# One fused block of two transformer layers plus a recurrent layer: start-up loads, first attention and the compression matmuls in another order

## The chip, the cores and the metric

The kernel runs on one core of a Trainium2 chip. The metric is the device time of one execution in microseconds (us), the median of several runs. TensorE (PE) does the matmuls and the transposes, VectorE (DVE) and ScalarE (ACT) the elementwise work, GpSimd (POOL) some of it, and the queues of SyncE (SP) and of ACT issue the transfers between HBM and the on-chip memory. All engines run their own instruction lists and meet at semaphores.

## The reference, cut to what matters

The input is 256 tokens of 1024 features, float32. The part that the change touches is the first mixer, `even_mixer`:

```
parts = split(hn @ w_in)           # q, kc, vc, ks, vs, kw, vw, g, dq, dk, dv
kc = compress_kv(kc, pos_k, w1_k, w2_k)    # 15 compressed keys and values per head group:
vc = compress_kv(vc, pos_v, w1_v, w2_v)    # gelu(window of 32 tokens @ w1) @ w2
gates = sigmoid(g)
o_a = nsa_attention(q, kc, vc, ks, vs, kw, vw, gates, bias)   # 8 heads, sum of three branches
o_b = diff_attention(dq, dk, dv, lam, subln_g, bias)          # 4 heads, rms_norm of the result
return concatenate([o_a, o_b]) @ w_out
```

Then come a squared-relu MLP, a second mixer (block attention, 16 heads), a second MLP, and a second block with a recurrence, another attention and a gated feed-forward. None of these is touched.

## The kernel before, in words

Every dense matmul is done in split precision. A weight slab of 1024 x 256 is loaded by SP into one of five places of `raw` (`RING = 5`); ACT copies it to `w_hi` in a rounded format (`split_hi`, L683), DVE subtracts to get `w_lo` (`split_lo`, L1023), and PE's `gemm` (L1561) does three products for each of 8 chunks and each of two halves: 48 matmuls for a slab, 6 for a chunk. ACT splits a slab three slabs ahead of its use (`AHEAD`), DVE two. The results lie in two PSUM buffers that alternate by group number. ACT or DVE must empty one before the second next group is written.

The first stage projects the normalised x by twelve slabs, in this order: KV_CMP, Q0, SKW, GATE, SV, DQ0, DK0, DQ1, DK1, DV0, DV1, Q1. GATE has 24 columns only. KV_CMP is the input of the compression, a chain of small float32 matmuls: two sets (k and v) of 16 with 45 columns each, then ACT's gelu, then three matmuls of `compress()`, then DVE's copies into `kc` and `vc`. Before, PE does the 16 of k behind the chunks of SV (two behind each), the 16 of v behind those of DQ0, and `compress()` after DK0.

The start: SP loads x, then the slabs up to SV, then the compression weights `cw1`, small things, and the slabs from DQ0 on. ACT's queue first issues the loads of `norm_mix`, of the bias table, and 18 small loads of parameters (`par_rows`, L765 and L767). Then it writes 16 copies of a row of bias values to HBM (L772), and when they have landed (`brow_out`) it loads from them the 2 MB tile `nb`, the bias of every head by query and key (L778): eight loads, each for the 16 partitions a, a+8, a+16, ... Behind those in ACT's order stands `root(0)` (L699), the square root for the first norm, on which DVE's `inv_rms` (L1035) and all evictions wait.

`attention(0)` is a loop over steps i with a software pipeline. In step i, PE does the transposes of pair i-2 (L1640), the values of pair i-3 (L1655), the scores of pair i (L1628), and then what the table `FILL` gives for the step: whole slabs or halves of slabs of the projections ("in"), or chunks of the output projection that are ready ("out"). DVE does `logits(i)` (L1063), then `normalise(i-1)` (L1092), and ACT the exponentials (L740) and the copies of the transposes (L723). There are 16 pairs in the first attention: for each of four head pairs two full ones (branches over all keys and over the window) and one compressed ("cmp", 15 keys), and four of the differential attention. Its rms_norm is done in steps 10 to 14 ("dn"): sums of squares on PE (L1674) and a square root on ACT in step 10, a reciprocal on DVE in step 11, 8 broadcasts on PE (L1685) in step 12, the product on DVE (L1105) and the split into high and low in steps 13 and 14.

Of the kernel before, what the change touches and what calls it, by code (L numbers as in the profile page):

```python
# [12 lines left out]
P = 128  # L13
# [35 lines left out]
    {0: [("in", DQ0, 0, 8)], 1: [("in", DK0, 0, 8)], 2: [("in", DQ1, 0, 8)], 3: [("in", DK1, 0, 8)], 4: [("in", DV0, 0, 4)],  # L49
     5: [("in", DV0, 4, 8)], 6: [("in", DV1, 0, 4)], 7: [("in", DV1, 4, 8)], 8: [("in", Q1, 0, 4)], 9: [("in", Q1, 4, 8)],  # L50
     14: [("out", 0, (0,)), ("out", 1, (0,))], 15: [("out", 0, (1, 4)), ("out", 1, (1, 4))],
     16: [("out", 0, (5, 6)), ("out", 1, (5, 6))], 17: [("out", 0, (7, 2)), ("out", 1, (7, 2))]},
# [12 lines left out]
IN_BEFORE = (5, 2, 6)  # L65
# [75 lines left out]
def build(nc, ctx, t, out):  # L141
# [210 lines left out]
    def att_pairs(p):  # L352
# [10 lines left out]
        if p == 0:  # L363
# [3 lines left out]
            def nsa(hp):  # L367
                heads, g = (2 * hp, 2 * hp + 1), hp // 2
                end, vg = CMP_BLOCK - 1, vc[:, g * HD:(g + 1) * HD]
                for b in range(2):  # L370
                    v = [sv[:, tb, b * P + g * HD:b * P + (g + 1) * HD] for tb in range(TB)]
                    pairs.append(dict(
                        kind="full", gate=8 * (b + 1) + 2 * hp, out=hp, start=(b == 0), stop=False, last=False,
                        units=[unit(aq[r, hp, :], skw[r, b, g, :], [nb[:, h, P:T], nb[:, h, :]])
                               for h, r in zip(heads, halves)],
                        pv=[full_pv(v)] * 2, qk_groups=(grp[Q0 if hp < 2 else Q1], grp[SKW]), v_groups=(grp[SV],)))
                pairs.append(dict(
                    kind="cmp", gate=2 * hp, out=hp, start=False, stop=True, last=True,
# [5 lines left out]
                    qk_groups=(g0 + CMP2_GROUP,), v_groups=()))  # L384
# [78 lines left out]
    def _(sp):  # L463
# [27 lines left out]
        for j in range(DQ0):  # L491
            a_slab(j)
        for i, name in enumerate(("k", "v")):
            sp.dma_start(cw1[:, i, :, :], t[f"ev_cmp_w1_{name}"][0].rearrange("(m p) j -> p m j", p=P)).then_inc(ld["cw"], 16)
        sp.wait_ge(xt, 4)
# [180 lines left out]
    def _(act):  # L676
# [31 lines left out]
        def attention(p, in_slab):  # L708
            a, pairs, probs_t = att[p], PAIRS[p], prob_ts[p // 2]
            n = len(pairs)  # L710
            for i in range(n + 3):
# [39 lines left out]
                if p == 0 and i == DN_STEP + 3:  # L751
# [8 lines left out]
        for name, (tile, row, n) in PARAMS.items():  # L760
            if name != "norm_mix":
                src, letters = t[name], " ".join("abcd"[:len(t[name].shape)])
                if len(src.shape) > 1:
                    src = src.rearrange(f"{letters} -> ({letters})")
                act.dma_start(prow[row:row + n, tile, :], src[0:n * P].rearrange("(r c) -> r c", c=P)).then_inc(ld["par"], 16)  # L765
        tail = t["conv_f_w_2"].rearrange("a b c -> (a b c)")[P * P:144 * P].rearrange("(r c) -> r c", c=P)
        act.dma_start(prow[CONV_F_TAIL[1]:CONV_F_TAIL[1] + 16, CONV_F_TAIL[0], :], tail).then_inc(ld["par"], 16)  # L767
# [14 lines left out]
        def a_slab(j, opens=True, closes=True):  # L782
# [11 lines left out]
            if j == DQ0:  # L794
                compress()
# [13 lines left out]
        for j in range(DQ0):  # L809
            a_slab(j)  # L810
        act.wait_ge(lam_ok, 1)
# [196 lines left out]
    def _(dve):  # L1008
# [42 lines left out]
        def attention(p, in_slab):  # L1051
# [889 lines left out]
```

## Time and profile before

| | |
|---|---|
| median of 3 runs | 1222.54 us (1221.37 to 1222.99) |
| the profiled execution | 1222.54 us, its span 1220.7 us, 1.8 us around it |
| busy: PE, DVE, ACT, POOL | 1155.7, 794.5, 587.8, 147.3 us |
| mean granted clock of TensorE | 0.969 |
| on the chain that ended last | PE 79%, DVE 10%, DMA 3%, ACT 3%, POOL 2% |

Times in the rows are microseconds from the start of the span. In a timeline or chain, a row is start, duration, engine, line, operation; "ACTq" and "SPq" are the queues that issue transfers, and a bracket at a row's end is the idle time ahead of it with what ended it. In a table of stretches the columns are busy time (and instructions) of PE, PE's weight loads, DVE, ACT and POOL, then the granted clock of TensorE as a share of 2.4 GHz, the share of the DMA engines, and GB/s. The span's first 180 us hold the part that the change touches.

### The profile page before, as it was taken

Reading aid. Unit: us, or ns where it says so; the run is one execution under the profiler, and the core shown is the slowest. Engines: PE = TensorE matmul, PEld = TensorE weight load, DVE = VectorE, ACT = ScalarE, POOL = GpSimd, SP = SyncE. Lnnn points to the kernel's source line nnn. Section 1 sums busy time; section 2 is a strip of 40 time slices with the busy share of each in tenths; the row PEclk is TensorE's granted clock in tenths of the full one; section 3 lists DMA queues with packets and bytes.
Section 4 is the critical chain, followed back from the end, with each engine's and each line's share of the span. In section 5 each row is a group of like instructions: output and inputs, shape, how many; then the busy total and the mean of one; then the engine's idle time right before and its main releaser. Section 6 shows DMA issues by size and latency. Waiting matters only on the chain.

```text
span 1220.7 us, 21634 instructions
## 1 busy us (share of the span) xinstructions
PE 1155.7 (95%) x9407; PEld 1111.2 (91%) x9407; DVE 794.5 (65%) x1131; ACT 587.8 (48%) x824; POOL 147.3 (12%) x83
## 2 busy tenths in 40 slices
PE   6899899999999999999999999999977979999997
PEld 5898679999998999999999989999975879999997
DVE  5647548775546565877543978875554678888842
ACT  4257645444334555444334465663354446665531
POOL 3000012000220003000022201400050030111000
PEclk9699799999999999999999999999988999999999
DMA  9733125655654544565565362555941444566550
GB/s 279 202 114 124 40 66 177 186 194 177 200 177 141 168 141 139 173 190 190 179 200 175 97 210 70 173 161 182 314 137 35 138 139 139 176 198 197 193 187 35
DMA packets 198770, 195.71 MB, mean 160 GB/s; under 512 B 9691, under 2 KB 196756, under 8 KB 198676
## 3 DMA queue, kind: packets, MB, share of 16 engines
q1 hardware_dynamic: 191360, 188.43, 48.6%
q10 hardware_dynamic: 7316, 5.91, 1.9%
q8 instruction: 74, 1.21, 0.4%
q14 instruction: 20, 0.16, 0.0%
HBM read 192.86 MB, written 1.46 MB: 159 GB/s over the span
## 4 chain that ended last, share of the span: by engine, by line
PE 79%; DVE 10%; DMA 3%; ACT 3%; POOL 2%; issue 2%; ACTq 1%; DVEq 0%; POOLq 0%
PE ps_gemm L1561 70%; PE ps_score L1628 2%; PE ps_out L1655 2%; DVE w_lo L1023 2%; PE ps_trans L1640 2%; DMA f_bias<-cum_scr 2%; PE ps_score L1850 2%; DVE prob L1063 1%; POOL f_bias L642 1%; DVE xc L1334 1%; DVE prob L1092 1%; ACTq L778 1%; PE ps_gemm L1726 1%; DVE rs L1035 1%; ACTq L765 1%
## 5 line engine op out<-in xcount | busy, mean ns | idle before, releaser
L1561 PE MATMUL ps_gemm<-act_hi,w_hi 128*128 128x256 f32 x1640 | 463.3, 284 | 19.1 <-ACT act_hi L957 6.7
L1561 PE MATMUL ps_gemm<-act_hi,w_lo 128*128 128x256 f32 x1640 | 458.3, 281 | 0.0
L1561 PE MATMUL ps_gemm<-act_lo,w_hi 128*128 128x256 f32 x1640 | 446.3, 281 | 0.0
L1023 DVE TENSOR_TENSOR w_lo<-raw,w_hi 128x2048 fp32r<-128x2048 f32 (+2 forms) x179 | 408.4, 2290 | 51.4 <-ACT w_hi L683 51.1
L683 ACT ACTIVATE w_hi<-raw 128x2048 fp32r<-128x2048 f32 (+2 forms) x179 | 332.6, 1862 | 187.6 <-DMA raw<-in_mlp_w 97.1
L1561 PEld LDWEIGHTS ps_gemm<-act_hi,w_hi 128*128 128x128 f32 x1640 | 311.2, 190 | 27.6 <-issue 17.5
L1561 PEld LDWEIGHTS ps_gemm<-act_hi,w_lo 128*128 128x128 f32 x1640 | 310.8, 190 | 0.2
L1561 PEld LDWEIGHTS ps_gemm<-act_lo,w_hi 128*128 128x128 f32 x1640 | 302.6, 188 | 1.5
L1561 PE MATMUL ps_gemm<-hid_lo,w_hi 128*128 128x256 f32 x512 | 143.1, 280 | 0.0
L1561 PE MATMUL ps_gemm<-hid_hi,w_lo 128*128 128x256 f32 x512 | 143.1, 280 | 0.0
L1561 PE MATMUL ps_gemm<-hid_hi,w_hi 128*128 128x256 f32 x512 | 142.8, 279 | 0.0
L1561 PEld LDWEIGHTS ps_gemm<-hid_lo,w_hi 128*128 128x128 f32 x512 | 96.2, 188 | 0.0
L1561 PEld LDWEIGHTS ps_gemm<-hid_hi,w_hi 128*128 128x128 f32 x512 | 96.0, 188 | 0.0
L1561 PEld LDWEIGHTS ps_gemm<-hid_hi,w_lo 128*128 128x128 f32 x512 | 95.9, 187 | 0.0
L740 ACT ACTIVATE prob<-prob,nmin 128x128 f32<-128x128 f32 (+3 forms) x128 | 54.3, 425 | 34.8 <-DVE nmin L1063 34.6
L608 POOL TENSOR_TENSOR sq_sum<-x 128x512 f32<-128x512 f32 x5 | 12.8, 2570 | 466.8 <-DVE x L1228 236.0
L828 ACT ACTIVATE hid_hi<-up_r 128x512 fp32r<-128x512 f32 x32 | 20.3, 634 | 93.3 <-DVE up_r L1246 93.3
L1561 PE MATMUL ps_gemm<-w_hi,act_hi 128*128 128x256 f32 (+1 forms) x192 | 57.4, 299 | 0.0
L1561 PE MATMUL ps_gemm<-w_lo,act_hi 128*128 128x256 f32 (+1 forms) x192 | 55.6, 290 | 0.0
L1561 PE MATMUL ps_gemm<-w_hi,act_lo 128*128 128x256 f32 (+1 forms) x192 | 55.6, 289 | 0.0
L1063 DVE CUSTOM_DVE_ANT_0 prob<-ps_score,bias 128x128 f32<-128x128 f32 (+1 forms) x96 | 25.6, 323 | 45.0 <-PE ps_score L1628 44.8
L1561 PE MATMUL ps_gemm<-w_hi,h_hi 128*128 128x256 f32 x192 | 53.1, 277 | 0.0
(282 smaller groups left out, 1733.4 us busy)
## 6 DMA issues: line engine op xcount, KB each, us to landing
raw<-in_mlp_w SPq DMA_DIRECT2D x64, 1024.0 KB, 5.3
raw<-in_w_in SPq DMA_DIRECT2D x30, 1024.0 KB, 5.5
raw<-in_w_up SPq DMA_DIRECT2D x24, 1024.0 KB, 5.3
raw<-in_od_w_in SPq DMA_DIRECT2D x12, 1024.0 KB, 5.1
raw<-in_w_down SPq DMA_DIRECT2D x12, 1024.0 KB, 5.3
raw<-in_ev_w_in SPq DMA_DIRECT2D x9, 1024.0 KB, 6.2
raw<-in_w_proj_a SPq DMA_DIRECT2D x8, 640.0 KB, 4.3
raw<-in_ev_w_out SPq DMA_DIRECT2D x4, 1024.0 KB, 5.5
```

Source lines behind the costliest of these rows:

```text
L608: ins = pool.tensor_tensor(dst, v, v, ALU.mult)
L642: link(pool.tensor_tensor(nb2[:, :, c0:c0 + n], nb2[:, :, c0:c0 + n], fcq[:, b, :].unsqueeze(2).to_broadcast([P, 16, n]), ALU.subtract))
L683: act.activation(w_hi[:, slot, 0:k, 0:n], raw[:, slot, 0:k, 0:n], ACT.Copy).then_inc(hi_done, 1)
L740: ins = act.activation(v, v, ACT.Exp, scale=-1.0, bias=nmin[:, k, b:b + 1], accum_out=psum_[:, k, b:b + 1])
L828: act.activation(hid_hi[:, 2 * j:2 * j + 2, :], up_r[:, j % 2, :, :], ACT.Square).then_inc(hid_h, 1)
L1023: dve.tensor_tensor(w_lo[:, slot, 0:k, 0:n], raw[:, slot, 0:k, 0:n], w_hi[:, slot, 0:k, 0:n].bitcast(F32), ALU.subtract).then_inc(w_ready, 1)
L1063: ins = dve.tensor_tensor_reduce(out=prob[:, k % PB, c0:c0 + w], in0=ps_s[:, m, c0:c0 + w], in1=u["bias"][b], scale=1.0, scalar=u["init"], ...
L1561: ins = pe.matmul(dst, lhs, rhs, start=(first and opens and i == 0), stop=(last and closes and i + 1 == len(order)), skip_group_check=True)
L1628: ins = pe.matmul(ps_s[:, m, c0:c0 + w], u["q"][:, b * P:(b + 1) * P], u["k"][b], start=True, stop=True)
L1640: ins = pe.transpose(ps_t[0:w, 0 if pr["kind"] == "diff" else m, q * P:(q + 1) * P], prob[:, k, c0:c0 + w], ident[:, :])
L1655: ins = pe.matmul(ps_o[r, pr["seq"] % 2, o0:o1], v, probs_t[0:k, m, c0:c1], start=(pr["start"] and q == 0), stop=(pr["stop"] and q == 1), ...
L1850: ins = pe.matmul(ps_s[:, j % 2, i * T:(i + 1) * T], gw[:, i, c, j - c + 1, :], xc[:, c, :], start=(q == 0), stop=(q == len(srcs) - 1))
```

## The change

It has five parts.

1. The 18 small loads of parameters go from ACT's queue to SP's, behind the slabs KV_CMP, Q0 and SKW; the two loads of `cw1` (1 MB each) now come ahead of the slabs GATE and SV.
2. The eight loads of `nb` are each for 16 neighbouring partitions.
3. All 32 small matmuls of the compression run behind the chunks of SV, four behind each. DQ0 is projected ahead of the attention, and `compress()` comes right after it (`IN_BEFORE` 5 to 6).
4. In the first attention the compressed pair of a head pair comes first of its three, not last. `FILL` is shifted: inputs in steps 0 to 8, outputs in steps 13 to 17.
5. The differential norm's reciprocal stands ahead of the logits of step 11 and its broadcasts are in step 11; what follows moves up a step.

```diff
@@ FILL, first attention
-    {0: [("in", DQ0, 0, 8)], 1: [("in", DK0, 0, 8)], 2: [("in", DQ1, 0, 8)], 3: [("in", DK1, 0, 8)], 4: [("in", DV0, 0, 4)],
+    {0: [("in", DK0, 0, 8)], 1: [("in", DQ1, 0, 8)], 2: [("in", DK1, 0, 4)], 3: [("in", DK1, 4, 8), ("in", DV0, 0, 4)],
...
-     14: [("out", 0, (0,)), ("out", 1, (0,))], 15: [("out", 0, (1, 4)), ("out", 1, (1, 4))],
-     16: [("out", 0, (5, 6)), ("out", 1, (5, 6))], 17: [("out", 0, (7, 2)), ("out", 1, (7, 2))]},
+     13: [("out", 0, (0, 1)), ("out", 1, (0, 1))], 14: [("out", 0, (4, 5)), ("out", 1, (4,))],
+     15: [("out", 1, (5, 6))], 16: [("out", 0, (6, 7)), ("out", 1, (7,))], 17: [("out", 0, (2,)), ("out", 1, (2,))]},
@@ sync
-        for j in range(DQ0):
+        for j in range(3):
             a_slab(j)
+        for name, (tile, row, n) in PARAMS.items():
...
+                sp.dma_start(prow[row:row + n, tile, :], src[0:n * P].rearrange("(r c) -> r c", c=P)).then_inc(ld["par"], 16)
...
         for i, name in enumerate(("k", "v")):
             sp.dma_start(cw1[:, i, :, :], ...).then_inc(ld["cw"], 16)
+        a_slab(GATE)
+        a_slab(SV)
@@ scalar
-        for a in (0, 4, 1, 5, 2, 6, 3, 7):
-            src = bass.AP(tensor=scr_w.tensor, offset=P - 1 - a, ap=[[16 * REL - 8, 16], [REL, 16], [1, T]])
-            act.dma_start(nb[a:P:8, :, :], src).then_inc(nb_in, 16)
+        for a in range(P // 16):
+            src = bass.AP(tensor=scr_w.tensor, offset=P - 1 - 16 * a, ap=[[16 * REL - 1, 16], [REL, 16], [1, T]])
+            act.dma_start(nb[16 * a:16 * a + 16, :, :], src).then_inc(nb_in, 16)
@@ vector, step i of the first attention, ahead of logits(i)
+                if p == 0 and i == DN_STEP + 1:
+                    g = st["a_in"].g0 + DN_GROUP
+                    dve.wait_ge(emptied[g % 2], out_count(g))
+                    dve.reciprocal(dn_rs[:, :], dn_sd[:, :]).then_inc(dn["r"], 1)
@@ tensor
-                if p == 0 and i == DN_STEP + 2:
+                if p == 0 and i == DN_STEP + 1:
                     pe.wait_ge(dn["r"], 1)
...
+        def compress_chunk(k):
...
+            for m in range(4 * (k % 4), 4 * (k % 4) + 4):
+                i = k // 4
                 ins = pe.matmul(ps_g[:, b, i * T:i * T + 3 * NC].rearrange("p (g c) -> p g c", g=3), cw1[:, i, m, :],
...
-        a_slab(SV)
+        a_slab(SV, between=compress_chunk)
+        a_slab(DQ0)
+        compress()
         pe.wait_ge(rst_ok, 1)
```

What stands in a row on PE around the first two chunks of SV, before (a chunk's last matmuls, the small ones of the compression, the next chunk):

```order
L1561 MATMUL ps_gemm<-w_lo,act_hi 128x256
L1726 MATMUL ps_gemm<-cmp_in,cmp_w_86 128x45 x2
L1561 MATMUL ps_gemm<-w_hi,act_hi 128x256
L1561 MATMUL ps_gemm<-w_hi,act_lo 128x256
L1561 MATMUL ps_gemm<-w_lo,act_hi 128x256
```

and after:

```order
L1564 MATMUL ps_gemm<-w_lo,act_hi 128x256
L1735 MATMUL ps_gemm<-cmp_in,cmp_w_86 128x45 x4
L1564 MATMUL ps_gemm<-w_hi,act_hi 128x256
L1564 MATMUL ps_gemm<-w_hi,act_lo 128x256
L1564 MATMUL ps_gemm<-w_lo,act_hi 128x256
```

The small matmuls of both sets are now inside SV; the slab DQ0 has none.

PE after the last chunk of the slab ahead of the attention's first step, before (the first scores are those of a full pair, and DQ0 is the fill):

```order
L1726 MATMUL ps_gemm<-cmp_in,cmp_w_86 128x45 x2
L1628 MATMUL ps_score<-a_skw,a_q 128x128 [waits emptied0,emptied1,rst_ok]
L1628 MATMUL ps_score<-a_skw,a_q 128x128
L1628 MATMUL ps_score<-a_skw,a_q 128x256 x2
L1561 MATMUL ps_gemm<-act_hi,w_hi 128x256 [waits emptied0,w_ready]
```

and after (end of DQ0, then `compress()`, whose result `kc` the first scores read):

```order
L1564 MATMUL ps_gemm<-act_hi,w_lo 128x256
L1747 MATMUL ps_gemm<-cmp_hid,cmp_w_94 128x30 [waits emptied1]
L1749 MATMUL ps_gemm<-cmp_w_94,cmp_hid 15x64 x2
L1631 MATMUL ps_score<-kc,a_q 128x7 [waits emptied1,rst_ok]
L1631 MATMUL ps_score<-kc,a_q 128x7
L1631 MATMUL ps_score<-kc,a_q 128x15 x2
L1564 MATMUL ps_gemm<-act_hi,w_hi 128x256 [waits emptied0,w_ready]
```

The first scores moved behind DQ0 and behind DVE's copies of the compressed keys.

## Rows read from the trace of the kernel before

**Rows 1.** The page, granted clock of TensorE in 40 slices, tenths.

```profile
PEclk9699799999999999999999999999988999999999
```

**Rows 2.** The chain that ended last, first 40 us: start, us, what.

```profile
2.13 0.62 ACTq L765
...
9.40 0.44 ACTq L767
...
12.37 5.76 DMA bias_wide_scr<-bias_row
18.15 0.63 ACTq L778
...
23.52 2.75 ACTq L778
...
28.10 1.76 DVE rs L1035
...
36.03 14.83 PE ps_gemm L1561 x96
```

**Rows 3.** Timeline of ACT, splits of slabs 0, 5, 6 and the gates.

```profile
11.17 1.91 ACT L683 ACTIVATE w_hi<-raw 128x2048 fp32r<-128x2048 f32 x1
...
43.87 1.91 ACT L683 ACTIVATE w_hi<-raw 128x2048 fp32r<-128x2048 f32 x1 [11.95 <-DMA raw<-in_ev_w_in]
46.78 1.91 ACT L683 ACTIVATE w_hi<-raw 128x2048 fp32r<-128x2048 f32 x1 [1.00 <-DMA raw<-in_ev_w_in]
50.92 1.28 ACT L705 ACT_TABLE_LOAD   x1 [2.23 <-PE ps_gemm L1561]
```

**Rows 4.** Timeline of SP's queue: the issue of slab GATE.

```profile
9.52 3.15 SPq L472 DMA_DIRECT2D raw<-in_ev_w_in  x1
```

**Rows 5.** Timeline of POOL: the mask on the bias tile.

```profile
41.20 2.09 POOL L620 TENSOR_SCALAR_AFFINE_SELECT bias<-bias 128x2048 f32<-128x2048 f32 x1 [22.06 <-DMA bias<-bias_wide_scr]
```

**Rows 6.** Busy time and granted clock by stretch, 31 to 60 us.

```profile
31.00:36.00 5.00, 0.15 (x1) 0.03 (x2) 4.88 (x10) 0.92 (x1) 0.00 (x0) 0.63 1.13 249
36.00:40.00 4.00, 3.97 (x22) 4.00 (x23) 3.81 (x16) 0.00 (x0) 0.00 (x0) 0.61 1.15 259
...
48.00:52.00 4.00, 4.00 (x20) 4.00 (x19) 3.77 (x7) 1.77 (x2) 0.00 (x0) 0.50 0.05 12
...
56.00:60.00 4.00, 4.00 (x22) 4.00 (x22) 0.00 (x0) 0.00 (x0) 0.00 (x0) 0.55 0.00 0
```

**Rows 7.** The chain through SV and DQ0, 52 to 75 us.

```profile
52.73 1.09 PE ps_gemm L1726 x4
53.81 1.42 PE ps_gemm L1561 x6
55.23 0.71 PE ps_gemm L1726 x4
...
59.98 0.75 PE ps_gemm L1561 x6
60.73 0.39 PE ps_gemm L1726 x4
...
64.58 0.86 PE ps_score L1628 x8
...
74.81 0.86 PE ps_score L1628 x8
```

**Rows 8.** The chain through the later steps of the first attention.

```profile
128.74 0.66 PE ps_trans L1640 x6
...
142.23 3.71 PE ps_gemm L1685 x16
...
173.36 0.61 PE ps_out L1655 x8
```

**Rows 9.** The page, DVE's splits and logits: busy, mean ns of one, idle before.

```profile
L1023 DVE TENSOR_TENSOR w_lo<-raw,w_hi 128x2048 fp32r<-128x2048 f32 (+2 forms) x179 | 408.4, 2290 | 51.4 <-ACT w_hi L683 51.1
...
L1063 DVE CUSTOM_DVE_ANT_0 prob<-ps_score,bias 128x128 f32<-128x128 f32 (+1 forms) x96 | 25.6, 323 | 45.0 <-PE ps_score L1628 44.8
```

More of the change, by code:

```diff
@@ L369, in nsa @@
                 end, vg = CMP_BLOCK - 1, vc[:, g * HD:(g + 1) * HD]
[L370 to L376, printed above, removed]
                 pairs.append(dict(
-                    kind="cmp", gate=2 * hp, out=hp, start=False, stop=True, last=True,
+                    kind="cmp", gate=2 * hp, out=hp, start=True, stop=False, last=False,
                     units=[dict(q=aq[r, hp, :], k=[kc[r, g, 0:NC0], kc[r, g, :]], blocks=[(0, NC0), (P, NC)],
@@ L383, in nsa @@
                     pv=[[(vg[0:NC0, :], NC0, (0, P), (0, P)), (vg[0:NC, :], NC, (P, T), (P, T))]] * 2,
-                    qk_groups=(g0 + CMP2_GROUP,), v_groups=()))
+                    qk_groups=(grp[Q0 if hp < 2 else Q1], g0 + CMP2_GROUP), v_groups=()))
+                for b in range(2):
+                    v = [sv[:, tb, b * P + g * HD:b * P + (g + 1) * HD] for tb in range(TB)]
+                    pairs.append(dict(
+                        kind="full", gate=8 * (b + 1) + 2 * hp, out=hp, start=False, stop=(b == 1), last=(b == 1),
+                        units=[unit(aq[r, hp, :], skw[r, b, g, :], [nb[:, h, P:T], nb[:, h, :]])
+                               for h, r in zip(heads, halves)],
+                        pv=[full_pv(v)] * 2, qk_groups=(grp[SKW],), v_groups=(grp[SV],)))
             def diff(h):
@@ L750, in attention @@
                         .then_inc(emptied[g % 2], 1)
-                if p == 0 and i == DN_STEP + 3:
+                if p == 0 and i == DN_STEP + 2:
                     for g in (st["a_in"].g0 + DN_GROUP + 1, st["a_in"].g0 + DN_GROUP + 2):
@@ L759, in _ @@
         act.dma_start(btab[:, :], t["bias_table"]).then_inc(ld["bias"], 16)
[L760 to L767, printed above, removed]
         split_hi(0)
@@ L793, in a_slab @@
                     if j == GATE else NS)
-            if j == DQ0:
-                compress()
         def compress():
@@ L1108, in attention @@
                     normalise(i - 1)
-                if p == 0 and i == DN_STEP + 1:
-                    g = st["a_in"].g0 + DN_GROUP
-                    dve.wait_ge(emptied[g % 2], out_count(g))
-                    dve.reciprocal(dn_rs[:, :], dn_sd[:, :]).then_inc(dn["r"], 1)
                 for part in FILL[p].get(i, ()):
@@ L1121, in attention @@
                         .then_inc(a["ol"], 1)
-                if p == 0 and i == DN_STEP + 4:
+                if p == 0 and i == DN_STEP + 3:
                     dve.wait_ge(dn["hi"], 1)
@@ L1178, in a_slab @@
             ins.then_inc(emptied[g % 2], 1)
-            if j == DK0:
-                compress()
         def compress():
@@ L1219, in _ @@
         ins.then_inc(lam_ok, 1)
+        a_slab(DQ0)
+        compress()
         dve.wait_ge(lam_e, 1)
@@ L1713, in _, with a_slab @@
         g0 = st["a_in"].g0
-        def a_slab(j, k0=0, k1=KS):
+        def a_slab(j, k0=0, k1=KS, between=None):
             s, g = st["a_in"].s0 + j, g0 + A_GROUPS[j]
-            gemm(s, g, act_hi, act_lo, before_chunk=x_in(0) if j == 0 else None, low_last=j == 0,
-                 between={SV: compress_k, DQ0: compress_v}.get(j), tok_major=j in (DV0, DV1, SV, GATE),
-                 n=GATES if j == GATE else NS, ks=range(k0, k1), opens=k0 == 0, closes=k1 == KS)
-            if j == DK0:
-                compress()
-        def compress_part(i, k):
-            b = (g0 + CMP1_GROUP) % 2
-            for m in (2 * k, 2 * k + 1):
+            gemm(s, g, act_hi, act_lo, before_chunk=x_in(0) if j == 0 else None, low_last=j == 0, between=between,
+                 tok_major=j in (DV0, DV1, SV, GATE), n=GATES if j == GATE else NS, ks=range(k0, k1), opens=k0 == 0,
+                 closes=k1 == KS)
+        def compress_chunk(k):
+            g = g0 + CMP1_GROUP
+            b = g % 2
+            if k == 0:
+                pe.wait_ge(emptied[b], gwait(g))
+                pe.wait_ge(ld["cw"], 16 * 6)
+                gi = g0 + A_GROUPS[KV_CMP]
+                pe.wait_ge(emptied[gi % 2], out_count(gi))
+            for m in range(4 * (k % 4), 4 * (k % 4) + 4):
+                i = k // 4
                 ins = pe.matmul(ps_g[:, b, i * T:i * T + 3 * NC].rearrange("p (g c) -> p g c", g=3), cw1[:, i, m, :],
@@ L1768, in _ @@
         a_slab(GATE)
-        a_slab(SV)
+        a_slab(SV, between=compress_chunk)
+        a_slab(DQ0)
+        compress()
         pe.wait_ge(rst_ok, 1)
```

24 lines of the change are left out of this document (10 added, 14 removed).

## The prediction, made before the changed kernel ran

> **What bounds the kernel now.** I read the page first: PE is the chain for four fifths of the span, and its granted clock is at full level nearly everywhere except in the second and the fifth slice (0.6 and 0.7), and twice late in the program [rows 1]. A slice is 30.5 us, so the two are 31 to 61 and 122 to 153 us, and that is where the change works. Behind the first attention, from some 178 us on, nothing differs, so the sum is made up to there.
>
> Next the chain of waits for the first 40 us [rows 2]. ACT's queue issues 18 parameter loads (2.13 to 9.84, first and last of 18 rows), the bias row goes to HBM and is back at 18.1, eight loads of the bias tile are issued until 26.3, and only then come ACT's table load and square root (1.8 us). DVE's reciprocal starts at 28.1, and PE starts slab SKW at 36.03, 7.9 us behind the root. PE had next to nothing to do from 31 to 36 [rows 6].
>
> Then the timeline of ACT from 40 us on [rows 3]. The splits of slabs 5 (DQ0) and 6 (DK0) start when their transfers land, at 43.87 and 46.78: up to there the DMA engines are the limit (their share is 1.1 in [rows 6]). The gates are evicted at 50.92, behind PE's slab GATE. They stand in ACT's order behind the split of DK0.
>
> Last the clock with the chain [rows 6, 7]. From 48 to 60 us PE is busy all the time, and still at 1.2 GHz or little over it. The slab before was GATE, whose products have 24 columns. In SV, 6 products of a chunk take 1.42 us and the 2 small matmuls behind them 0.71 us (4 records); at 59.98 the same are 0.75 and 0.39 us. So the clock came back about 7 us into SV, where dense work is two thirds of the time at the low clock.
>
> **Part 1, the start.** ACT is rid of 18 issues, 7.7 us, but could not have used much of it: the split of slab 0 begins at 11.17 [rows 2, 3], the bias row is written by DVE at 12.3 behind PE, and the write to HBM issues at 12.37 all the same. What can change is its landing (5.76 us, beside SP's slabs) and the issue of the eight loads: six take 0.63 each, the last 2.75 as its queue is full [rows 2]. Eight times 0.64 would be 5.1 us instead of 8.1. So the root comes between 0 and 4 us earlier (1 for the landing, 3 for the issue), I take 2: SKW starts at about 34.
>
> This does not reach the gates. The issue of parameters on SP, 18 times 0.43 or 7.7 us, now stands between SKW and `cw1`. SP's queue is blocked by its backlog at 9.5 [rows 4], so that the DMA engines have work for some 6 to 7 us more; then they run short for about 1.3 us. All bytes up to DK0 are the same, thus DK0 lands at 46.78 + 1.3 = 48.1. Its split 1.9, table load 1.28, gates 0.45: 51.8. The first small matmul of the compression needs the buffer of GATE; it ran at 52.73 [rows 7]. Gain 0.9 us. The bounds: 3.9 if the DMA engines never run short and the new shape of the bias loads lets the slabs land 1.7 earlier, minus 3 if that shape hinders them.
>
> The mask on the bias ended at 43.3 [rows 5]; the first logits move to about 82 us, so the bias tile itself has 35 us of cover.
>
> **Part 2, the compression inside SV.** At the low clock a chunk of SV becomes 1.42 + 2 x 0.71 = 2.84 us: half of the time is dense, where it was two thirds. Before, the clock stayed down for 7 us of the denser mix. I take it that it stays down for all of SV: from the first small matmul on, 8 x 1.42 (small) + 7 x 1.42 = 21.3 us, against 64.58 - 52.73 = 11.85. That is +9.45. DQ0 is then without small matmuls: 8 x 0.75 = 6.0 at the full clock, 11.4 at the low. It begins low and recovers inside; I take 7.3 (a recovery after some 3 us of dense work, as behind 36 us, where the stretch 36 to 40 has a mean of 0.61 [rows 6]). Before it took 74.81 - 64.58 - 0.86 = 9.37. That is -2.07.
>
> Two waits are new. DQ0 writes the buffer that SV leaves, which ACT empties in 0.84 us; before, the scores of 0.86 us lay there: +1.0. The first scores read `kc`, which DVE copies behind the eviction of DQ0: +0.6. `compress()` itself is in both.
>
> The Trainium skill, page "TensorE: Matmul & The Clock Gate", section "What's actually happening", says that activity releases the throttle and that a sustained busy stretch brings the full clock. Taken by PE's busy time alone, SV (no gaps) would be at 2.4 GHz early; the row for 48 to 60 us shows PE busy without a gap at 0.50 to 0.55, so here the rule holds only if dense work counts. That is the second rival.
>
> **Part 3, the attention.** In steps 0 to 8 PE does the same less DQ0, with one short step: step 2 has half a slab (4 chunks of 0.75 and some 1.3 us of the pairs' own matmuls) against DVE's logits (four of 0.32), about as much for the normalisation, and a split of 2.29 [rows 9], 5.0 us: +0.7. Unfilled steps are four in both (10 to 13 before, 9 to 12 after), and both have the same products. The reciprocal ahead of the logits of step 11 is no stall: the square root is ready about when PE's scores of that step are. The 8 broadcasts (3.71 us at the low clock [rows 8]) now lie beside the logits of a full pair, where they cost less. But step 15 has 12 matmuls (1.5 us) against 2.8 of DVE (logits and normalisation): +1.3, and the clock falls a step sooner, in step 10. Before, steps 10 to 18 took 128.74 to 173.97 [rows 8]. I take +2.0 for all of this, with -2 and +4 as ends.
>
> **Sum.** -0.9 + 9.45 - 2.07 + 1.0 + 0.6 + 2.0 = +10.1 us. The profiled execution took 1222.54 us, which is the median too: 1232.6 us.
>
> **The rivals.**
> *The clock comes back in SV* as it did before, 7 us in. Then SV is 6.8 us at the low clock, a third of its 21.3, and two thirds of 11.6 us (15 groups at 0.75 to 0.78) at the full one: 14.6, +2.75 for +9.45. DQ0 is 6.0, -3.4. The sum is -0.9 + 2.75 - 3.4 + 1.6 + 2.0 = +2.0: 1224.6 us. For it: the mix of SV and DQ0 kept its short times from 59.98 on, up to the end of DQ0 [rows 7]. Against it: that was a clock already up, and a denser mix.
>
> *Faster.* The same, and the start is passed on: DK0 lands early, gates are ready with PE, 3.5 us for 0.9, and the attention's last steps gain 1.5 rather than lose 2, since the clock falls less there than in the fifth slice before. 1222.5 + 2.0 - 2.6 - 3.5 = 1218.4 us. For it: PE had 5 idle us at 31 to 36. Against: the landings.
>
> *The new shape of the bias loads hinders the slabs.* The eight loads took from 18.15 to 41.2 for 2.1 MB, 91 GB/s, beside the slabs [rows 2, 5]. If each now holds up the other queue, DK0 lands 4 us later, on top of the forecast: 1236.6 us. It decides from 1.8 us on, as the gates have little less in hand than this. The Trainium skill, "SBUF — State Buffer", section "Door 1: The DMA port swizzle", says that 16 neighbouring partitions reach four ports (104 GB/s at 1 MiB), where strided ones reach more. By that rule alone the eight need 20 us, not more than they took; only the crowding would cost.
>
> **How the numbers follow.** Forecast 0.54, clock back in SV 0.20, faster 0.16, hindered 0.10. A difference of 0.2% (2.4 us) is what can be told from none. The forecast and the last are slower; the second is around the edge, most of it within; so faster 0.18, same 0.18, slower 0.64. The range holds the second case and most of the faster: 1217 to 1238 us. The forecast's own is 1228 to 1236.
>
> **What would show it.** In the table of stretches, PE's granted clock through SV (about 52 to 73 us) at 0.50 with PE busy; the first small matmul at 51 to 53 us; SKW started at 33 to 35; the first scores near 83 us, where before those of step 1 were at 74.81 [rows 7]; a DMA share under 1 for a moment near 17 us. Wrong would be a clock of 1.00 before 62 us, a first small matmul outside 49 to 55, or a length of the attention off by more than 4 us from the sum of part 3.

## The result: 1241.55 us, 1.6 to 1.8% slower

The changed kernel took 1241.55 us (median of 4 runs, 1241.38 to 1241.62), against 1222.0 us before (median of 4): 1.6% more. The ratio on record, 1.0178 (interval 1.0165 to 1.0193), takes in all 29 executions of the changed kernel: 24 further ones took 1241.8 to 1246.7 us, and the median of all is 1244.1. The forecast was 1232.6 us and its range ended at 1238. The direction was right and the size was outside the range. In the profiled executions (1222.54 and 1240.8 us) the span grew from 1220.7 to 1239.0 us. Both kernels have 9407 matmuls, so the 18.3 us are waits and a lower clock. Read first the granted clock of the page, beside that of before [rows 1]:

```profile
PEclk9659989999999999999999999999988998999999
```

The second slice stayed at 0.6, the third (62 to 93 us) fell to 0.5, where it had been 0.9. The fifth rose. So the loss is in the first 95 us, and a little comes back later.

Why is the clock low for so long? First, all of it begins late. ACT's timeline gives the splits of slabs DQ0 and DK0 and the table load of the gates, as in [rows 3]:

```profile
56.93 1.91 ACT L694 ACTIVATE w_hi<-raw 128x2048 fp32r<-128x2048 f32 x1 [6.32 <-DMA raw<-in_ev_w_in]
59.94 1.91 ACT L694 ACTIVATE w_hi<-raw 128x2048 fp32r<-128x2048 f32 x1 [1.10 <-DMA raw<-in_ev_w_in]
61.87 1.28 ACT L716 ACT_TABLE_LOAD   x1
```

Both slabs land 13.1 us later than before (43.87 and 46.78). The table load stands behind DK0's split in ACT's order; before, it came 2.2 us behind that split, released by PE, and now it follows at once. So the landing of DK0 sets the eviction of the gates, and this frees the buffer that the first small matmul of the compression writes. SP's queue shows what it did meanwhile (start, us, then the load that it issued):

```profile
9.05 2.79 SPq L499 DMA_DIRECT2D par_rows<-in_norm_mlp  x1
...
20.97 0.52 SPq L501 DMA_DIRECT2D par_rows<-in_conv_f_w  x1
...
23.01 9.67 SPq L503 DMA_DIRECT2D cmp_w<-in_ev_cmp_w_v  x1
32.73 8.07 SPq L473 DMA_DIRECT2D raw<-in_ev_w_in  x1
40.85 3.51 SPq L486 DMA_DIRECT2D raw<-in_ev_w_in  x2
44.40 1.19 SPq L509 DMA_DIRECT2D cmp_w<-in_ev_cmp_w_k  x2
...
48.48 0.43 SPq L512 DMA_DIRECT2D small<-in_b_forget  x1
48.95 8.66 SPq L473 DMA_DIRECT2D raw<-in_ev_w_in  x4
```

The parameter loads occupy SP for 12.4 us (9.05 to 21.49). GATE, which was issued at 9.52 before [rows 4], is issued at 32.73; DQ0 at 48.95. The table of stretches (busy time of PE, PEld, DVE, ACT, POOL, then granted clock, DMA share and GB/s) shows what the DMA engines did with it:

```profile
16.00:20.00 4.00, 4.00 (x33) 4.00 (x33) 4.00 (x7) 0.00 (x0) 2.46 (x2) 0.92 0.62 97
20.00:30.00 10.00, 8.33 (x64) 7.62 (x63) 9.80 (x13) 3.56 (x3) 0.00 (x0) 1.00 1.16 122
...
48.00:52.00 4.00, 4.00 (x21) 4.00 (x20) 2.20 (x9) 1.91 (x1) 0.00 (x0) 0.50 0.24 50
...
72.00:76.00 4.00, 4.00 (x21) 4.00 (x21) 0.00 (x0) 0.00 (x0) 0.00 (x0) 0.50 0.00 0
...
92.00:96.00 4.00, 3.31 (x34) 3.12 (x32) 1.19 (x5) 0.00 (x0) 0.00 (x0) 1.00 0.09 11
```

There are two different losses here. At 16 to 20 and 48 to 52 us the engines had little to do (share 0.62 and 0.24). From 20 to 30 us they were fully busy (1.16) and moved 122 GB/s, while before moved, in the same stretch and also fully busy:

```profile
20.00:30.00 10.00, 9.65 (x77) 8.99 (x75) 5.48 (x7) 3.69 (x4) 0.00 (x0) 1.00 1.11 272
```

The chain from the first small matmul to the first scores (start, us, what), beside [rows 7]:

```profile
63.67 1.94 PE ps_gemm L1735 x8
65.61 1.42 PE ps_gemm L1564 x6
67.03 1.57 PE ps_gemm L1735 x8
...
84.94 1.57 PE ps_gemm L1735 x8
86.51 8.12 PE ps_gemm L1564 x48
...
95.78 0.62 PE ps_score L1631 x8
```

Eight chunks, each of six wide matmuls at 1.42 us and eight small ones at 1.57 us, none at the short times that [rows 7] has from 59.98 on: 22.84 us at a clock of 0.50, with PE busy without a gap (72 to 76 us above).

**The ledger**, by the prediction's own terms. The attention ends where the output slab's first matmul starts, at 177.77 us before and 197.93 after, a difference of 20.2 us.

| term | before | after | difference | predicted |
|---|---|---|---|---|
| start to first small matmul | 52.73 | 63.67 | +10.9 | -0.9 |
| from there through SV | 11.85 | 22.84 | +11.0 | +9.45 |
| DQ0 and the waits up to the scores | 9.37 + 0.47 for `compress()` | 9.27 | -0.6 | -0.47 |
| attention, to the output slab | 103.35 | 102.15 | -1.2 | +2.0 |
| behind it, to the end of the span | 1042.93 | 1041.07 | -1.9 | 0 |

The attention's 103.35 us of before is 177.77 less 74.81, the scores of step 0 (0.86) added, and the 0.47 of `compress()` taken off, as that now lies ahead.

### The profile page after: what moved, and what is told of

Its sections match the earlier page's. It is cut to its first block, busy times and chain, and to the rows that moved or that the text cites. A ratio compares the mean times of both kernels' runs of the same rounds, so it can differ in the third digit from the quotient of the medians.

```text
span 1239.0 us, 21636 instructions
## 1 busy us (share of the span) xinstructions
PE 1162.6 (94%) x9407; PEld 1121.0 (90%) x9407; DVE 797.5 (64%) x1131; ACT 586.8 (47%) x823; POOL 146.5 (12%) x83
## 3 DMA queue, kind: packets, MB, share of 16 engines
q1 hardware_dynamic: 191940, 188.62, 48.1%
## 4 chain that ended last, share of the span: by engine, by line
PE 78%; DVE 8%; SPq 5%; DMA 4%; ACT 3%; POOL 2%; issue 1%; ACTq 0%; DVEq 0%; POOLq 0%
PE ps_gemm L1564 68%; PE ps_out L1658 2%; PE ps_score L1631 2%; PE ps_trans L1643 2%; DMA f_bias<-cum_scr 2%; DVE w_lo L1026 2%; PE ps_score L1848 1%; DVE prob L1066 1%; PE ps_gemm L1735 1%; SPq L549 1%; POOL f_bias L653 1%; DMA raw<-in_w_in 1%; SPq L499 1%; SPq L503 1%; DMA raw<-in_ev_w_in 1%
## 5 line engine op out<-in xcount | busy, mean ns | idle before, releaser
L751 ACT ACTIVATE prob<-prob,nmin 128x256 f32<-128x256 f32 (+3 forms) x128 | 54.3, 425 | 42.9 <-DVE nmin L1066 42.7
```

The costliest lines, as they stand in the source:

```text
L751: ins = act.activation(v, v, ACT.Exp, scale=-1.0, bias=nmin[:, k, b:b + 1], accum_out=psum_[:, k, b:b + 1])
```

## The experiments

Theories: **P**, the place of the bias loads in the tile slows all transfers beside them. **O**, SP's order starves the DMA engines. **M**, small matmuls between the chunks keep the clock down. Each run is timed against runs of before on the same chip; its ratio is the one on record, over all executions of both kernels, with a 95% interval (it can differ by some 0.1% from the quotient of the two medians). The runs were made on four chips, so a comparison of two changed kernels is best made by their ratios. Executions of one kernel spread over up to 11.5 us, and a trace shows only one of them. In the expectations, O1 and O2 are two halves of O (the parameter loads; `cw1` and the nine small loads ahead of DQ0), A says that the terms simply add, and T that a stretch of low clock is only moved to another place.

### P: the bias loads

Put back alone in the changed kernel:

```
-        for a in range(P // 16):            # nb[16a : 16a+16]
+        for a in (0, 4, 1, 5, 2, 6, 3, 7):  # nb[a : 128 : 8]
```

> The changed kernel with the eight bias loads as before (16 partitions, 8 apart). Theory P, the place of the partitions: loads for 16 neighbouring partitions hold the whole traffic at some 122 GB/s (stretches 20 to 30 us of the changed kernel), and that makes DK0 land 13 us late. Then the DMA rate from 20 to 30 us is 230 GB/s or more, the first small matmul of the compression runs at 52 to 55 us rather than 63.7, and the time falls by 8 to 11 us, to 1231 to 1234. Rival O, the order of SP's list (18 small loads and 2 MB of cw1 ahead of GATE and SV): the time stays at 1240 to 1242. SV at the low clock stays in both.

Measured: 1234.93 us, ratio 1.012 (1.0084 to 1.0155). The first small matmul at 57.63, 6.0 us earlier; DK0's split at 53.90. All three numbers stay behind those of theory P (a start at 52 to 55, 230 GB/s, 1231 to 1234 us); theory O is what is left to explain. From 20 to 30 us:

```profile
20.00:30.00 10.00, 9.17 (x73) 8.56 (x72) 8.48 (x10) 3.56 (x3) 0.00 (x0) 1.00 1.11 220
```

The opposite, the kernel before with nothing but the new shape of the loads:

> The kernel before with the bias loads alone changed to 16 neighbouring partitions. Theory P: DMA rate near 125 GB/s while they run, DK0 lands about 10 us late, the first small matmul at about 62 us, and the time is 1228 to 1232, since SV and DQ0 keep their mix and only the start is late. Rival O: no difference, 1221 to 1224.

Measured: 1226.98 us, ratio 1.0042 (1.0021 to 1.0062); the first small matmul at 59.08, 6.35 us later (about 9 were expected). The total lost less than the start, 5 us, since SV and DQ0 needed about 1 us less. Where before moved 272 GB/s:

```profile
20.00:30.00 10.00, 9.76 (x80) 9.34 (x78) 4.07 (x6) 2.08 (x3) 0.00 (x0) 1.00 1.13 209
```

So the new loads cost 6 us of the start in both kernels. Is it that the partitions are neighbours, or which ones a load reaches? The next run takes partitions two apart, within a range of 31:

```
+        for a in (0, 64, 32, 96, 1, 65, 33, 97):   # nb[a : a+31 : 2]
```

> The changed kernel with each bias load for 16 partitions 2 apart (span of 31), the order of the loads alternating between the halves. Theory P in the form of ports: a span of 31 partitions reaches as many ports as 16 partitions 8 apart, so this is as fast as with a distance of 8, 1231 to 1234, DMA rate over 220 GB/s from 20 to 30 us. If it is that neighbouring rows are read from HBM, or nearness in general, it is in between or as slow as the changed kernel, 1236 to 1242.

Measured: 1237.27 us (1.0134, 1.0092 to 1.0176), first small matmul at 57.53, the same as with partitions eight apart. The total lies in the range of the rival (1236 to 1242), but its interval overlaps that of the run with partitions eight apart, and the start and the rate are as theory P had them:

```profile
20.00:30.00 10.00, 9.69 (x77) 9.09 (x77) 8.42 (x10) 3.56 (x3) 0.00 (x0) 1.00 1.12 241
```

The two spread shapes move 220 and 241 GB/s at the same share at which neighbours move 122. The Trainium skill, page "SBUF — State Buffer", section "Door 1: The DMA port swizzle", fits: by its table 16 neighbours reach four ports, and both of the spread shapes eight. That the slabs of the other queue pay as well, the prediction had only as a rival. Ports as the cause remain an argument: both spread shapes also issue their loads in another order (the halves of the tile in turn), and shape and order were not separated.

### O: SP's order

Three kernels divide it. All have the bias loads put back. The first also has the parameter loads on ACT's queue again; the second keeps them on SP, and has GATE and SV ahead of `cw1` and the nine small loads behind DK0; the third undoes both parts on loads, so that only the compression, DQ0's place and the attention's order are left of the change.

```
 sp:  x, 3 slabs,         cw1, GATE, SV, small loads, DQ0, ...     (1)
 sp:  x, 3 slabs, params, GATE, SV, cw1, DQ0, DK0, small loads ... (2)
 sp:  x, 3 slabs,         GATE, SV, cw1, small loads, DQ0, ...     (3)
```

> The strided-bias kernel (first small matmul 57.6, DQ0 landed 50.9, DK0 53.9, total 1234.9), with the 18 parameter loads back on ACT's queue; SP still issues cw1 ahead of GATE and SV. Theory O1 (the 9 to 12 us in which SP issues the parameter loads, with 100 GB/s or less moving from 16 to 20 us, are what is left of the lateness): DK0 lands at 49 to 50.5, first small matmul at 53 to 54, total about 1231, although the root comes later again. Rival O2 (cw1 and the small cmp_w and lam_v loads that SP issues ahead of DQ0, with nothing in flight, are what is left): DK0 lands within 1 us of 53.9 and the total stays at 1234 to 1235.5.

Measured: 1231.4 us (1.0092, 1.006 to 1.0124). DK0's split:

```profile
47.90 1.91 ACT L686 ACTIVATE w_hi<-raw 128x2048 fp32r<-128x2048 f32 x1 [1.10 <-DMA raw<-in_ev_w_in]
```

> The strided-bias kernel, parameter loads still on SP behind slab SKW, but GATE and SV issued ahead of cw1 again, and the nine small loads (cmp_w second layer, lam_v, forget bias: 4.5 us of SP's time) behind DK0 rather than ahead of DQ0. Theory O2: DK0 lands 4 to 5 us earlier than 53.9, at 49 to 50, first small matmul 53 to 54, total about 1231. Theory O1 (the parameter loads hold it): DK0 gains under 1.5 us, total 1233.5 or more. It could also lose: GATE earlier on the queue means the weight of GATE lands before cw1, and the small matmuls may wait for cw1 instead (by the before trace they did not: cw1 had landed long before 52.7).

Measured: 1232.32 us (1.0101, 1.0073 to 1.0129):

```profile
49.53 1.91 ACT L696 ACTIVATE w_hi<-raw 128x2048 fp32r<-128x2048 f32 x1 [1.12 <-DMA raw<-in_ev_w_in]
```

The first small matmul stood at 51.63 in the one and at 53.25 in the other, against 57.63. I had set O1 and O2 as rivals, and each mend alone brings back what is left: they don't exclude each other. (The second kernel has two edits, the place of `cw1` and that of the nine small loads; which of them did it was not separated.) SP issues its loads one by one, and in these traces the time that it spends on small ones was lost only where nothing large was in flight (share 0.24 at 48 to 52 us above). It could be saved at either end.

> The kernel after, with the two parts of the change that touch loads undone: SP issues GATE and SV ahead of cw1 and the parameter rows are loaded from ACT's queue, as before, and the bias loads take every eighth partition. What is left of the change is the compression in SV, DQ0's place and the attention's order. If the terms simply add (theory A): first small compression matmul back at 52.7 (52 to 53.5; after 63.7), SV 22.8 us at a clock of 0.50 as after, first scores at 84.8, total 1241.5 less 10.9 = about 1230.6 (1229.5 to 1231.5). Rival: the 11 us of the SV stage were only as long because the late start had let TensorE idle before it; with the early start the clock comes back inside SV as it did before (at about 58), SV takes 16 to 18 us, and the total is 1224 to 1226.

Measured: 1232.96 us (1.0099, 1.0069 to 1.013), span 1231.1. The chain:

```profile
52.94 1.93 PE ps_gemm L1735 x8
54.88 1.42 PE ps_gemm L1564 x6
...
74.22 1.57 PE ps_gemm L1735 x8
75.78 7.96 PE ps_gemm L1564 x48
```

Start 52.94, SV 22.84, first scores 84.89: theory A to 0.2 us in each. The rival, that SV was slow only because PE had idled ahead of it, is out: here PE idled 0.41 us ahead of the first small matmul, as in the kernel before, and then had 22.84 us without a gap at 0.50. The total was 2.4 us over the 1230.6 expected, and its median above the range; but that sum started from 1241.5, and from the 1244.1 of all executions it gives 1233.2.

### M: the small matmuls

The old mixture, two calls (four records) behind each chunk, `k` in SV and `v` in DQ0, put into the changed kernel:

```
         a_slab(SV, between=compress_chunk)
-        a_slab(DQ0)
+        a_slab(DQ0, between=lambda k: compress_chunk(k, 1))
...
-            for m in range(4 * (k % 4), 4 * (k % 4) + 4):
-                i = k // 4
+            for m in (2 * k, 2 * k + 1):                 # i is 0 (k) in SV, 1 (v) in DQ0
```

ACT then has to empty DQ0's buffer ahead of its part of `compress()`, and does.

> The changed kernel with the small matmuls of k behind SV's chunks and those of v behind DQ0's, two each, DQ0 still ahead of the attention. Theory M, the mix keeps the clock down: SV is 11.5 to 15 us rather than 22.8, as the clock comes back inside it, DQ0 about 9.4 rather than 8.1, and compress() now waits some 2.3 us for ACT's gelu: 7 to 8 us less, 1233 to 1235. Rival, the clock is down for the long wait ahead of SV and not for the mix: SV is 11.5 + the same total of low time, less than 3 us gained, 1239 to 1242.

Measured: 1241.9 us (1.017, 1.013 to 1.021), no gain that can be told beside the changed kernel's 1.0178: a total in the rival's range, though theory M was right about SV: the clock came back inside it, and the first scores came at 90.86, 4.9 us earlier. Then it went again:

```profile
68.00:72.00 4.00, 4.00 (x20) 4.00 (x21) 0.82 (x1) 0.00 (x0) 0.00 (x0) 0.50 0.00 0
72.00:76.00 4.00, 4.00 (x32) 4.00 (x32) 0.00 (x0) 0.00 (x0) 0.00 (x0) 0.84 0.00 0
...
88.00:92.00 4.00, 1.84 (x15) 1.65 (x16) 0.69 (x4) 2.93 (x5) 0.00 (x0) 0.79 0.82 264
92.00:96.00 4.00, 4.00 (x19) 4.00 (x20) 2.75 (x9) 3.06 (x9) 0.00 (x0) 0.50 0.00 0
```

With `v` in DQ0, the hidden layer, the second step and the copies of `kc` and `vc` have nothing to hide behind, PE is busy 1.84 of 4 us from 88 to 92, and the next slab runs at 0.50. The output slab began at 198.06, as in the changed kernel (197.93): the rest was lost between 150 and 170, where the clock stood at 0.50 for longer.

> The strided-bias kernel with the small matmuls split: k behind SV's chunks, v behind DQ0's, two per chunk, as the kernel before had them mixed. In the run with the changed bias loads this brought the first scores 4.9 us forward (90.9 against 95.8) and the total nothing (1241.9 against 1241.55), because stretches at a clock of 0.50 came at 88 to 98 and 148 to 162 instead. Theory T (the low clock is only moved: what is not lost at the small matmuls is lost at the next place where TensorE waits): scores at about 85, total 1233.5 to 1236 against 1234.9. Rival (that run was an accident of where the waits fell): total 1229.5 to 1231.

Measured: 1230.66 us (1.0096, 1.0065 to 1.0126); against the kernel without the mixture (1.012) the intervals overlap, so although the median is within the rival's range, this one decides little. Its first scores came at 84.66.

> The same kernel with its small matmuls split as before (k behind SV's chunks, v behind DQ0's, two per chunk). What is left of the change is then DQ0 ahead of the attention, the second compression step right behind DQ0 instead of behind DK0, and the attention's order. First small matmul 52.9; clock back at about 60; SV with its part 8.5 us + 4.4, DQ0 with its part 8.9: the last small one at about 75, first scores at 78.5 to 79.5 (before: 64.6, with DQ0 and the v part then still to come). If the order of the attention is worth the 1 to 2 us that the spans of before and after suggested: total 1218 to 1221 beside a before of about 1220. Rival T (the low clock is only moved, since TensorE now waits about 3 us for kc and vc behind the split compression): a stretch at 0.50 behind the first scores, total 1224 to 1227.

Measured: 1228.06 us (1.005, 1.0028 to 1.0073), above both forecasts; scores at 82.22 and not at 79, as the clock came back only at 67.16.

> Split small matmuls again, with cw1 ahead of GATE on SP, parameter rows on ACT's queue and the bias loads strided (that order gave the first small matmul at 51.6, 1.1 us ahead of before). Theory: the numbers of the run beside it, less 1.1 to 1.3 us. Rival T as there: total 1223 to 1226.

Measured: 1228.57 us (1.0049, 1.0031 to 1.0068), scores at 77.10. The start 2.2 us ahead of its neighbour's is not in the median. The two traces don't match these medians: the profiled executions took 1229.23 and 1224.26 us, and differ by 5.0 us, as the first scores do (82.22 and 77.10). Both kernels stay slower than before, and both are above T's forecast. What they have and before has not are the 4.3 us, most of them idle, from the end of DQ0's last wide matmul to the first scores (1.14 us in the changed kernel), with a low stretch behind it (0.50 from 76 to 80 us in the second). No run tests whether that is the cause.

Then the mixture was not thinned but taken out:

```
-        a_slab(SV, between=compress_chunk)
+        a_slab(SV)
+        for k in range(KS):
+            compress_chunk(k)
```

> The kernel with only the compression, DQ0's place and the attention's order changed (small matmuls from 52.9, SV 22.84 us at a clock of 0.50 throughout, first scores 84.9, total about 1231 to 1233), with its 64 small matmuls taken out from between SV's chunks and set in one block behind SV's last chunk. Theory M (it is the mixture, eight small matmuls behind every six large ones, that holds the clock at 0.50): the dense slab brings the clock back some 5 us after its start, as it did before with two small ones per chunk, SV's 48 large matmuls take about 8.5 us, the block of small ones 6.3 us at full clock, 15 us in all, first scores at about 77, total 7 to 8 us lower, about 1224. If the small ones by themselves drop it again: 8.5 + 12.6 = 21 us, and the total gains 1 to 2 us. Rival (the clock follows what TensorE did before 52, not the mixture): 22 to 23 us again.

Measured: 1224.63 us (1.0022, 0.9997 to 1.0047), 8.3 us under the same kernel with the mixture (by the ratios 0.8%); first scores at 78.19, 6.7 us earlier. Here T does not hold: the gain reached the total.

```profile
61.12 7.87 PE ps_gemm L1735 x64
69.00 8.05 PE ps_gemm L1564 x48
...
78.19 0.62 PE ps_score L1631 x8
```

The block of 64 takes 7.87 us, not the 6.3 expected, and DQ0 behind it 8.05 us (5.85 for a slab at full clock): the mean clock is 0.90 from 64 to 68 us and 0.50 from 68 to 72. Still it pays. In the changed kernel itself, loads and all:

> The kernel after with nothing changed but the 64 small matmuls in one block behind SV's last chunk. With the late start (63.7) kept, theory M: SV 14 to 16.5 us instead of 22.8, first scores at 88 to 89.5 instead of 95.8, total 1234 to 1235.5. Rival (TensorE idled before SV, and after that idle time the clock needs longer to come back than in the run that started early): SV 19 to 21 us, total 1238 to 1240.

Measured: 1231.76 us (1.0087, 1.0068 to 1.0105), 9.8 us under the changed kernel (by the ratios 0.9%), more than I expected.

```profile
66.56 10.11 PE ps_gemm L1735 x64
76.67 7.49 PE ps_gemm L1564 x48
...
85.29 0.62 PE ps_score L1631 x8
```

Its first scores are 10.5 us earlier, and this has two causes. In the changed kernel, the timeline of PE has 4.98 us of idle time inside SV, ahead of the first small record, released by the eviction of the gates:

```profile
63.67 1.94 PE L1735 MATMUL ps_gemm<-cmp_in,cmp_w 128*128 128x45 f32 x8 [4.98 <-ACT gates L716]
```

With the block, SV's chunks do not wait for it (first wide matmul at 58.64, clock back at 63.43). So the mixture had also tied SV to the buffer of GATE, and through ACT's order to the landing of DK0. From SV's first wide matmul to DQ0 it is 29.45 us in the changed kernel and 18.03 with the block: 11.4 us less, of which 5.0 are that wait and 6.4 the clock. (This trace's SV began 1.6 us later, which takes a part of it back.)

> The change with all that the runs blamed taken out: parameter rows on ACT's queue, cw1 ahead of GATE on SP, bias loads for every eighth partition, and the 64 small matmuls in one block behind SV. If the three prices add: 51.6 + 16.2 + 9.1 = first scores at 76.9 and a total 1.2 us under the run with the block alone (1224.6), 1223 to 1224 (ratio 1.001 to 1.002). Rival: the three overlap (the blocks of low clock move), total 1225 to 1227.

Measured: 1219.44 us (0.999, 0.9975 to 1.0005), better than both forecasts: first scores at 74.63, 2.3 us earlier than the sum. With loads and mixture mended, what is left of the change costs nothing and gives nothing that can be measured beside before. But this kernel also has the `cw1` order and the block, which before has not; beside the kernel that adds just these to before (the last one below), it is slower.

### A version that beats both

Order (1) let the first small matmul come at 51.6, a little ahead of before. In the kernel before, `cw1` ahead of GATE is the whole edit:

> The kernel before with one thing changed: SP issues cw1 ahead of GATE and SV. Theory O: the first small matmul stood at 51.6 with this order (DK0 landed 47.9, the root ended near 25.3 instead of 28.3), so the total gains about 1.1 us: 1218.5 beside 1219.6. Rival: GATE's weight lands 5 us later (32.6) and DK0's 1 us later, and the clock, not the loads, decides: within 0.5 us of before, or 1 us slower.

Measured: 1219.23 us, ratio 0.9979 (0.9956 to 1.0002). Repeated, as the interval reached over 1:

> The kernel before with cw1 ahead of GATE and SV on SP, once more, against more runs of before, because its ratio of 0.9979 [0.9956, 1.0002] left open whether it is faster. Theory O: the first small matmul 1.1 us earlier, so 0.998 to 0.9995. Rival: nothing, 0.9995 to 1.002.

Measured: 1219.07 us, 0.9989 (0.9974 to 1.0004). A gain of 0.1 or 0.2% is possible, and not shown. Then, in the same kernel, the blocks:

```
-                 between={SV: compress_k, DQ0: compress_v}.get(j),
+            if j in (SV, DQ0):       # behind the slab's last chunk
+                for k in range(KS):
+                    (compress_k if j == SV else compress_v)(k)
```

> The kernel before with cw1 ahead of GATE on SP, and its small matmuls no longer between chunks: the 32 for k in one block behind SV's last chunk, the 32 for v in one block behind DQ0's. Theory M: a dense slab brings the clock back sooner than one with small ones between its chunks (2.7 us after SV's first wide matmul in the run with one block of 64; 4.6, 6.4 and 12.5 us in three runs with two per chunk for each chain, four records), so SV gains 1 to 2 us, and blocks of 32 are short enough (about 4 us) not to drop it: total 1217 to 1219, 1 to 2 us under the run of the same kernel with the small ones between. Rival: even a block of 32 takes the clock down again, as the 64 did at their end (67.3, DQ0 then at 0.50), which costs 4 us for each: 1222 to 1227.

Measured: 1215.79 us (1212.72 to 1217.57), ratio 0.9956 (0.994 to 0.9973): faster than before, 3.3 us under the same kernel without the blocks, and 2.2% under the changed one by the ratios.

```profile
55.81 3.52 PE ps_gemm L1731 x32
...
60.61 6.82 PE ps_gemm L1563 x48
67.42 3.52 PE ps_gemm L1731 x32
70.94 0.86 PE ps_score L1630 x8
71.80 5.85 PE ps_gemm L1563 x48
```

The scores of step 1 come at 70.94, where they stood at 74.81 [rows 7]. A block of 32 takes 3.5 us; the clock dips behind the first (0.62 from 60 to 64 us), and DQ0 takes 6.82 us; behind the second it does not, and the next slab takes 5.85.

This kernel is also 3.65 us under the mended one (1219.44 us, 0.999, 0.9975 to 1.0005), timed on the same chip. The two have the same order of loads and no mixture; they differ in DQ0's place, in one block of 64 or two of 32, and in the attention's order. So the rest of the change, with its block of 64, does cost 0.3%; which part of it does was not tested.

What the mixture does to the clock, in all the traces. "Back" is the first wide matmul of under 0.30 us in the timeline of PE, counted from SV's first wide one. The idle time ahead of the first small record is counted in: 0.4 us in the first four traces of the second row, 2.5 in the fifth, 5.3 to 6.0 in the third row. Each number is of one execution.

| small records between chunks | kernels | clock back after, us |
|---|---|---|
| 8 | the changed one, and five more | not within SV, which takes 22.84 us in each |
| 4 | before; cw1 first, twice; mixture with order (3), with (1) | 9.3; 7.1, 11.5; 15.5, 11.2 |
| 4 | before with the new bias loads; mixture in the changed kernel, and with strided bias loads | 12.0; 16.1, 16.8 |
| 0 | block of 64 with order (3), changed kernel, mended; blocks of 32 | 2.9, 4.8, 5.0; 5.2 |

The six kernels of the first row have their own control: in DQ0, which follows without small records, the clock is back after 3.3 to 5.3 us.

## Why the prediction was wrong

**The start** is the step that failed: "they run short for about 1.3 us ... thus DK0 lands at 46.78 + 1.3 = 48.1". DK0's split began at 59.94, and the first small matmul stood at 63.67 for 51.8. The step counted bytes and took the rate for given. Two things were wrong in it, each shown by putting it back. The rate: with the new shape of the bias loads both queues together move 122 GB/s from 20 to 30 us, and 220 without it; this costs 6.0 us in the changed kernel and 6.35 in the one before. The rival had it, with 4 us and a chance of 0.10; as the shape was new, no row of before could give its price. The pauses: the step looked at the parameter loads alone, and found one. SP's list has a second place where only small loads are issued, between SV and DQ0 (44.40 to 48.91). Before, they lay behind a backlog; after, the queue had run dry by then. With both parts put back the first small matmul stands at 52.94. The order of SP's list costs 4.7 us beside the 6.0 of the bias loads.

SKW did start at about 34, as predicted (33 to 35), but by luck: two errors cancelled. ACT's square root ended at 22.67, so that DVE's reciprocal, at 28.10 before [rows 2], could follow 5.4 us earlier, more than the 2 taken (the eight issues took 3.99 us for the 5.1 of the forecast); then PE waited for the parameter rows, the very loads that had been moved:

```profile
33.40 0.89 PE L1760 MATMUL ps_trans<-ident,par_rows 128*128 128x128 f32 x4 [4.23 <-DMA par_rows<-in_conv_f_w]
...
46.82 0.36 PE L1564 MATMUL ps_gemm<-w_hi,act_hi 128*128 128x24 f32 x1 [5.41 <-DVE a_q L1180]
```

The edit that freed ACT's queue gave its gain to the next wait. The second line is one more wait: DVE's eviction stood behind the split of GATE, which was landing late.

**SV** was right in its mechanism: the clock stays down for all of it, at the same 1.42 us for a chunk. Its size was 11.0 for 9.45: eight small records take 1.57 us, not 2 x 0.71 = 1.42, and the first eight 1.94; over eight groups these are the 1.5 us. The run with the early start has the same 22.84 us, and the runs with a block have the clock back within 5.2 us, so the mixture does this and not what PE did before it. One reading was wrong: the prediction has PE busy without a gap from 48 to 60 us, but in the kernel before it idled 0.41 us ahead of the first small matmul:

```profile
52.00:56.00 4.00, 3.59 (x17) 3.30 (x17) 0.00 (x0) 2.46 (x4) 0.00 (x0) 0.50 0.81 262
```

The changed kernel shows what was wanted there, a long stretch at 0.50 with no gap at all. The rival of a clock that comes back in SV, at 0.20, did not occur in any of the six kernels with eight small records a chunk.

**DQ0 and its waits**: -0.6 for -0.47, right as a sum, and that is luck. DQ0 itself took 8.12 us, not 7.3, as the clock came back only 5.2 us into it. The wait of 1.0 us for SV's buffer did not occur (PE was busy 4.00 of 4 us from 84 to 88, where DQ0 begins). From DQ0's end to the scores it was 1.14 us, for 0.6 and `compress()`.

**The attention** was +2.0 in the forecast and -1.2 in the trace. The split of step 15 and the short step 2 were priced, and their single rows were not compared. The difference itself can't be told from none: with the same attention, the stretch from the first scores to the output slab was 102.2 us in the changed kernel, 103.4 in that of order (3), 102.2 there with the block, and 104.6 in the changed kernel with the block. These differ by the places where the clock falls between 130 and 170 us, which shift from kernel to kernel; the share of the pairs' order alone was not isolated.

**The sum**: the forecast's error is 9.0 us, 1241.55 for 1232.6. The two profiled executions differ by 18.3 us, 8.2 more than the 10.1 forecast: +11.8 from the start, +1.5 from SV, -0.1 from DQ0, -3.2 from the attention and -1.9 from behind it. The last 0.8 us are what the median lies above the profiled execution. For the -1.9 I have no cause.

## What to carry to other kernels

A list of loads on one queue is a schedule: before a load is moved, go through it for each place where only small loads would be issued, and ask what large transfer is in flight then. The byte count says when a slab can land only if the rate stays, and the shape of one load sets the rate of its neighbours too. And where small matmuls are to fill in, try them in blocks behind a wide slab rather than between its chunks: it was worth 8 to 10 us in two kernels here (against eight records between chunks), and 3 us in the kernel before (against four), where the intervals of the two just fail to overlap (0.994 to 0.9973, 0.9974 to 1.0004; the first timing of the kernel without blocks reached down to 0.9956).

## What the runs showed of the hardware

- The DMA engines were busy at much the same share (1.11 to 1.16) and moved 122, 220, 241 or 272 GB/s. Their busy share did not tell the rate.
- PE busy without a gap ran for 23 us at 1.2 GHz with eight small records (45 columns) behind each six wide ones, and came back to 2.4 GHz within 2.9 to 5.3 us when the slab was wide only. With four, it took 7.1 to 16.8 us, idle time inside the slab included, and differently in two runs of one kernel (7.1 and 11.5). The Trainium skill, page "TensorE: Matmul & The Clock Gate", section "What's actually happening", has it that activity releases the throttle; here 22.84 us of PE's busy time alone did not, and the measurement decides.
- In a block of 64 small records the clock fell (7.9 to 10.1 us for the block, in three kernels), and the next slab took 7.5 to 8.1 us, where it takes 5.85 at 2.4 GHz. Behind two blocks of 32, which took 3.5 us each, it took 6.8 and 5.85.
- The 18 parameter loads took 7.7 us of ACT's queue at the start and 12.4 us of SP's behind the slabs, where two of them waited about 3 us each for the backlog.
